# Feed-forward of a two-layer trunk: gate and up by seven half-size block products on two halves of the tokens, with block sums formed in PSUM

## The chip, the cores and the metric

One core of a Trainium2 chip. The metric is device microseconds of one execution; three runs of the kernel before gave 3630.57, 3633.33 and 3633.56, a median of 3633.33.

## The reference

Two layers over 1024 prompt frames and 8 × 16 sample frames, T = 1152 tokens of D = 1024. Layer 0 mixes tokens with RWKV-7, layer 1 with chunked band attention. After each mixer comes the part that is changed:

```python
def swiglu_ffn(x, w_gu, w_down):
    gate, up = jnp.split(x @ w_gu, 2, axis=-1)
    return (jax.nn.silu(gate) * up) @ w_down
# every layer: x += mixer(rmsnorm(x)); x += swiglu_ffn(rmsnorm(x), ...)
```

w_gu is 1024 × 5632 and w_down 2816 × 1024, all float32.

## The kernel before

Phases follow one another: front, recurrence, project, feed-forward 0, attention, feed-forward 1. Tokens lie along the free axis. Every float32 product is made of three fp32r matmuls: an operand is split into a high part (a cast, on ScalarE) and a low part (value less high part, on GpSimd for weights and VectorE for tokens), and `PASSES` multiplies high·high, high·low, low·high. A matmul has a 128 × 128 weight and 384 token columns, a third of T.

`ffn_phase` goes over the 22 blocks of 128 hidden rows, one a turn. Block 0 is plain (`plain_third`: 8 k-tiles × 3 passes × 3 thirds for gate and for up, 144 matmuls), partly while the last third of the norm is still made. In a turn g of the other 21, gate and up of one block are a 2 × 2 block product: rows are gate and up, the inner dimension is two halves of D, columns are two of the thirds. Strassen's scheme needs 7 products of 4 k-tiles × 3 passes; the last third is plain and needs 4. So a turn has 11 × 12 = 132 matmuls. Weight sums (units 2, 3, 5, 8) are made by GpSimd, token sums T1 to T4 once, in `first_turn`. Block sums are taken from PSUM to SBUF (s1, s17) and added by VectorE. Between the products stand the down projection of the block before: 8 `down_tile`s of 3 passes × 3 thirds (72 matmuls, 3 banks), each followed by one VectorE add of 128 × 1152 into H (`add`, L2393). The silus are ScalarE's, the product with up VectorE's, and the hidden block is split again (hid). The last turn has no down tiles; a tail of 24 tiles × 6 matmuls (L2255) makes the down products of the last two blocks and feeds the next phase. The order on each engine is written out by hand; engines meet by semaphores, and each runs its list in order.

Of the kernel before, what the change touches and what calls it, by code (L numbers as in the profile page):

```python
# [23 lines left out]
P = 128  # L24
# [5 lines left out]
CW = T // 3  # L30
DFF = 2816
# [1897 lines left out]
def ffn_phase(nc, t, mem, o, layer):  # L1929
# [5 lines left out]

    TURNS = HB - 1
    SA, SB, SC, TG, TU, DOWN = 0, 1, 2, 3, 4, 5
    A11, A12, A21, A22, DW = 0, 1, 2, 3, 4
    with ExitStack() as ctx:
        sem = phase_semaphores(nc, ctx, f"ffn_{layer}")  # L1940
        raw_in = [sem(f"raw_in{u}") for u in range(6)]
        u_hi, u_lo, u_done, d_hi, d_lo = (sem(x) for x in ("u_hi", "u_lo", "u_done", "d_hi", "d_lo"))
        sum_ready, sp_passed, pool_passed = sem("sum_ready"), sem("sp_passed"), sem("pool_passed")
        down_done, added = sem("down_done"), sem("added")
        s1_ready, s16_ready, s17_ready, c22_ready, c21_ready, c12_ready = (sem(x) for x in
            ("s1_ready", "s16_ready", "s17_ready", "c22_ready", "c21_ready", "c12_ready"))
        silu1_ready, silu2_ready, silu3_ready, h1_ready, h2_ready, h3_ready = (sem(x) for x in
            ("silu1_ready", "silu2_ready", "silu3_ready", "h1_ready", "h2_ready", "h3_ready"))
        hh_ready, hid_part, hid_ready, last_hi, last_lo = (sem(x) for x in ("hh_ready", "hid_part", "hid_ready", "last_hi", "last_lo"))
        gate_done, up_done, b12_read = sem("gate_done"), sem("up_done"), sem("b12_read")  # L1950
        xf_ready, tf_ready, t_hi, t_lo = (sem(x) for x in ("xf_ready", "tf_ready", "t_hi", "t_lo"))
# [8 lines left out]
        U_AT, D_AT = ((4, 5, 0, 1), (2, 3)) if layer == 0 else ((0, 1, 2, 3), (4, 5))  # L1960
        TAIL_BANK = (5, 0, 3, 4, 1, 2) if layer == 0 else (0, 3, 1, 2)
        TAIL_FREE = {0: (silu1_ready, TURNS + 2), 3: (silu3_ready, TURNS + 1), 4: (h3_ready, TURNS + 1),
                     1: (c21_ready, TURNS + 1), 2: (c12_ready, TURNS + 1), 5: (added, 8 * TURNS - 7)}
# [7 lines left out]
        def x(rows, third):  # L1971

            return tuple(mem.xs[:, part, 4 * rows:4 * rows + 4, third * CW:(third + 1) * CW] for part in range(2))
# [11 lines left out]
        def _(sp):  # L1985
# [10 lines left out]
            for q in range(2):  # L1996
                load_down(q, 0)
# [3 lines left out]
            for n, slots in ((7, (A11, A21, A22)), (8, (A12,))):  # L2001
                sp.wait_ge(u_lo, n)
                for slot in slots:
                    load_gu(slot, 2)
# [1456 lines left out]
```

## Time and profile before

| | before |
|---|---|
| median of 3 runs | 3633.33 us (3630.57 to 3633.56) |
| the profiled execution | 3635.54 us, of which the span is 3633.8 |
| PE, DVE, ACT, POOL busy | 94%, 48%, 35%, 47% of the span |
| granted TensorE clock, mean | 0.979 |
| feed-forward 1, first product to tail | 2850.27 to 3589.61 us |

PE is the TensorE matmul, PEld its weight load, DVE VectorE, ACT ScalarE, POOL GpSimd. The span is from the first to the last instruction. A busy share is an average over phases; which wait ends last in a phase is read from its rows.

### The profile page before, as it was taken

The page shows a single profiled execution, that of the slowest core. Times are in us where ns is not written, and L with a number is a line of the kernel's source. Part 1 is how long each engine was busy: PE and PEld are TensorE (multiplying, and loading weights), DVE is VectorE, ACT ScalarE, POOL GpSimd, SP SyncE. Part 2 cuts the span into 40 slices and gives each one's busy share as a digit, 9 for nine tenths or more (in the row PEclk, how much of TensorE's full clock was granted, in tenths as well). Part 3 has the DMA queues.
Part 4 walks back from the last instruction along what each step waited for, and adds up shares of the span by engine and source line. Part 5 has one row for each costly group of instructions (what it writes and reads, how often), then busy time and mean ns, then how long its engine had stood idle before and what let it go on. Part 6 is the DMA issues. An engine that isn't in the chain of part 4 may idle for free. (4 is left out here: it accounts for less than half of the span.)

```text
span 3633.8 us, 85950 instructions
## 1 busy us (share of the span) xinstructions
PE 3404.7 (94%) x34270; PEld 3155.9 (87%) x34270; DVE 1755.0 (48%) x3081; ACT 1265.7 (35%) x2607; POOL 1703.8 (47%) x1482
## 2 busy tenths in 40 slices
PE   8999878888886999999999999999989999999999
PEld 7999767777775989999999887777769899999998
DVE  6212457766663374454445533333343744545444
ACT  5212444454442132222222334444443322222224
POOL 5444355554551544445455544344433444454544
PEclk9999899999997999999999999999999999999999
DMA  4422101111102211111111134444441111111111
GB/s 151 155 87 86 65 23 38 38 45 44 42 18 92 89 44 46 46 40 51 35 52 41 60 99 101 110 102 88 105 105 65 42 48 46 40 49 37 52 38 69
DMA packets 420929, 234.94 MB, mean 65 GB/s; under 512 B 189668, under 2 KB 394228, under 8 KB 419751
## 3 DMA queue, kind: packets, MB, share of 16 engines
q1 hardware_dynamic: 417074, 216.57, 21.3%
q10 hardware_dynamic: 3572, 14.33, 1.0%
q8 instruction: 211, 3.46, 0.4%
q14 instruction: 72, 0.58, 0.1%
HBM read 188.28 MB, written 47.80 MB: 65 GB/s over the span
## 5 line engine op out<-in xcount | busy, mean ns | idle before, releaser
L2124 PE MATMUL ps<-xs,split 128*128 128x384 f32 x4032 | 738.9, 334 | 0.0
L2044 POOL TENSOR_TENSOR split<-work,split 128x512 fp32r<-128x512 f32 x320 | 409.7, 1291 | 676.2 <-ACT split L2269 676.2
L2124 PEld LDWEIGHTS ps<-xs,split 128*128 128x128 f32 x4032 | 703.0, 188 | 0.0
L2393 DVE TENSOR_TENSOR H<-ps,H 128x1152 f32<-128x1152 f32 x320 | 433.9, 1356 | 495.6 <-PE ps L2138 495.4
L2138 PE MATMUL ps<-split,split 128*128 128x384 f32 x2880 | 554.7, 336 | 11.7 <-DVE split L2467 11.0
L2138 PEld LDWEIGHTS ps<-split,split 128*128 128x128 f32 x2880 | 506.8, 189 | 13.0 <-DVE split L2467 11.7
L1228 PE MATMUL ps<-arena 64*64 64x64 f32 (+2 forms) x8800 | 428.0, 236 | 51.0 <-DVE arena L1654 15.5
L2269 ACT CAST split<-work 128x512 fp32r<-128x512 f32 x320 | 194.6, 620 | 585.5 <-PE ps L2124 349.4
L1228 PEld LDWEIGHTS ps<-arena 64*64 64x64 f32 x8800 | 323.2, 136 | 86.3 <-issue 34.0
L2939 PE MATMUL ps<-xs,split 128*128 128x384 f32 x1656 | 361.3, 355 | 2.6 <-POOL split L2853 2.6
L601 PE MATMUL ps<-mixed,wsplit_mix 128*128 128x384 f32 x1872 | 333.4, 340 | 10.6 <-DVE mixed L813 10.2
L601 PEld LDWEIGHTS ps<-mixed,wsplit_mix 128*128 128x128 f32 x1872 | 330.5, 190 | 13.2 <-DVE mixed L813 12.8
L1222 PE MATMUL ps<-arena 64*64 64x64 f32 (+2 forms) x5632 | 305.8, 241 | 28.8 <-DVE arena L1659 14.4
L2939 PEld LDWEIGHTS ps<-xs,split 128*128 128x128 f32 x1656 | 277.8, 190 | 30.1 <-issue 22.4
L1222 PEld LDWEIGHTS ps<-arena 64*64 64x64 f32 x5632 | 244.9, 134 | 63.4 <-DVE arena L1659 28.0
L2124 PE MATMUL ps<-split,split 128*128 128x384 f32 x1512 | 282.5, 336 | 0.0
L2124 PEld LDWEIGHTS ps<-split,split 128*128 128x128 f32 x1512 | 263.9, 188 | 0.0
L3102 ACT ACTIVATE work<-work,work 128x640 f32<-128x640 f32 (+3 forms) x144 | 101.1, 702 | 279.7 <-DVE work L3193 272.1
L2905 POOL TENSOR_SCALAR work<-work,work 128x640 f32<-128x640 f32 (+2 forms) x64 | 95.0, 1484 | 189.4 <-DVE work L3198 189.4
L1197 POOL TENSOR_TENSOR arena<-arena 128x320 f32<-128x320 f32 (+2 forms) x144 | 123.6, 866 | 127.2 <-PE ps L1228 102.1
L2852 POOL TENSOR_SCALAR split<-work 128x256 fp32r<-128x256 f32 x104 | 88.7, 853 | 181.2 <-DMA work<-in_attn_w_qkv 141.8
L3193 DVE CUSTOM_DVE_ANT_0 work<-ps,work 128x640 f32<-128x640 f32 (+3 forms) x144 | 91.7, 661 | 168.2 <-PE ps L2984 136.5
(316 smaller groups left out, 5189.6 us busy)
## 6 DMA issues: line engine op xcount, KB each, us to landing
work<-in_ffn_w_gu SPq DMA_DIRECT2D x168, 256.0 KB, 3.1
work<-in_ffn_w_down SPq DMA_DIRECT2D x88, 256.0 KB, 2.9
work<-in_cache_v SPq DMA_DIRECT2D x64, 256.0 KB, 3.9
work<-in_cache_k SPq DMA_DIRECT2D x256, 64.0 KB, 2.2
rkv_scratch<-lora ACTq DMA_DIRECT2D x24, 576.0 KB, 2.8
stage_mix<-in_rwkv_w_rkv SPq DMA_DIRECT2D x24, 512.0 KB, 3.7
work<-in_attn_w_qkv SPq DMA_DIRECT2D x24, 512.0 KB, 4.1
h_scratch<-H SPq DMA_DIRECT2D x2, 4608.0 KB, 12.5
```

What stands on the lines that cost most here:

```text
L601: last = pe.matmul(mem.ps[:, 4 * v + c, 0:CW], mem.wsplit[:, v, w, k * P:(k + 1) * P], mixed[part][:, k, c * CW:(c + 1) * CW], start=(k == ...
L1197: pool.tensor_tensor(m.lt[:, n % 2, 0:G, :], m.at[:, slot_of(pr, g), 0:G, 0:64], spread(m.level[:, l, :], G), ALU.mult).then_inc(lt_ready, 1)
L1222: last = pe.matmul(out[lo:hi], lhsT[lo:hi], rhs[lo:hi] if rhs is not None else eye(lo, hi), start=start, stop=stop)
L1228: last = pe.matmul(out[to:end], lhsT[lo:hi], rhs[lo:hi] if rhs is not None else eye(lo, hi), start=start, stop=stop)
L2044: pool.tensor_tensor(w[:, 1, :], UNIT_SOURCE[i], w[:, 0, :].bitcast(F32), ALU.subtract).then_inc(u_lo, 1)
L2124: last = pe.matmul(bank(b), w[:, part, k * P:(k + 1) * P], operand[xpart][:, k, :], start=(first and k == 0 and a == 0), stop=(k == 3 and ...
L2138: last = pe.matmul(bank(DOWN + c), w[:, part, (k % 4) * P:(k % 4 + 1) * P], third(mem.hid[:, xpart, :], c), start=(a == 0), stop=(a == 2))
L2269: act.copy(unit(i)[:, 0, :], UNIT_SOURCE[i]).then_inc(u_hi, 1)
L2393: dve.tensor_tensor(by3(mem.H[:, k, :]), mem.ps[:, DOWN:DOWN + 3, 0:CW], by3(mem.H[:, k, :]), ALU.add).then_inc(added, 1)
L2905: pool.tensor_scalar(pr, pr, mem.rinv[:, N % 2, 1:2], None, ALU.mult).then_inc(np_ready, 1)
L2939: last = pe.matmul(ps[:, GEMM + b, 0:CW], mem.wsplit[:, (3 * p + u) % 2, w, k * P:(k + 1) * P], mem.xs[:, part, k, c * CW:(c + 1) * CW], s ...
L3102: act.activation(pr, pr, ACT.Exp, scale=-1.0, bias=mem.mx[:, N % 2, h:h + 1], accum_out=mem.rsum[:, N % 2, h:h + 1]).then_inc(ex_ready, 1)
```

## The change

Both feed-forward phases are rewritten; nothing else is. The tokens are cut into two halves of 576, and each half product is done in two quarters of 288 columns. Gate and up of a block are then 7 products (P1 to P7, units 1 to 7) of 2 quarters × 4 k-tiles × 3 passes, 168 matmuls of 288 columns, and no plain third remains. The first two blocks are plain (`plain_third`, then `plain_block`, both with 384 columns), and 20 turns follow. In a turn P1 starts bank pair SA; ScalarE copies it from PSUM to bank pair SB (copied_b) while P2 accumulates onto SA; P3 accumulates onto SB, ScalarE copies SB to SC (copied_c), P4 accumulates onto SB, ScalarE copies SB to SA (copied_a), P5 accumulates onto SA, P6 starts SA anew, P7 accumulates onto SC. VectorE forms c22 and c12 from these and s, the copy of P6 in SBUF (p5_copied), and the hidden values as m0 (first half) and m1 (second half), both by quarters c = 0, 1. One matmul step is one k-tile of a quarter, 3 matmuls; down tiles are now 32 of 3 matmuls with 288 columns, in two banks by turns, spread over 44 of the 56 steps, and VectorE adds each to H (128 × 288). The weight units have 3 slots for 4, the down weights come in four pieces of 256 columns through one raw buffer (high_down, low_down), for two of 512. Token sums are T1 to T4 of 4 × 576, made in `plain_block`'s time in two parts each (`value`, `combine`, `t_high`, `t_low`; a part is 128 × 1152). s2_s4 and s3_s1 are the weight sums on GpSimd.

```diff
-    TURNS = HB - 1
-    SA, SB, SC, TG, TU, DOWN = 0, 1, 2, 3, 4, 5
-    A11, A12, A21, A22, DW = 0, 1, 2, 3, 4
+    TURNS = HB - 2
+    A11, A12, A21, A22 = 0, 1, 2, 3
+    GATE, UP = (0, 1, 4), (2, 3, 5)
+    SA, SB, SC, DOWN = 0, 2, 4, 6
...
+        UNIT_AT = {1: 1, 2: 2, 3: 0, 4: 1, 5: 0, 6: 2, 7: 0}
...
+            def s2_s4(g):
+                hold(pool, pool_passed, p_done, product_no(0, g))
+                hold(pool, pool_passed, sum_ready, 4 * g - 2)
+                pool.tensor_tensor(unit(3)[2], mem.raw[:, A22, :], mem.raw[:, A11, :], ALU.subtract).then_inc(sum_ready, 1)
...
+            with pool.Fori(1, TURNS) as g:
+                s2_s4(g)
+                low(3, g)
+                low(4, g)
+                low(6, g)
+                low_down(2, 4 * g + 3)
+                low(5, g)
+                low_down(3, 4 * g + 4)
                 low(1, g + 1)
...
+                s3_s1(g + 1)
+                low(7, g)
+                low_down(0, 4 * g + 5)
+                low(2, g + 1)
...
+            def down_tile(j, g):
+                m, q = down_at(j)
+                if j in (0, 4):
+                    pe.wait_ge(hid_ready, 2 * g + 1 + j // 4)
+                if j % 8 == 0:
+                    pe.wait_ge(d_lo, 4 * g + j // 8 + 1)
+                pe.wait_ge(added, TILES * g + j + 1)
+                w = mem.dring[j // 8 % 2]
                 for a, (part, xpart) in enumerate(PASSES):
...
+                    last = pe.matmul(qbank(DOWN + j % 2), w[part][:, (m % 2) * P:(m % 2 + 1) * P], quarter(mem.hid[xpart], q), start=(a == 0), stop=(a == 2))
                 last.then_inc(down_done, 1)
...
+            def plain_block():
+                step, done = 0, 0
+                for n in range(4):
+                    w, rows = mem.ring[PLAIN_AT[n]], n % 2
+                    pe.wait_ge(u_lo, n + 1)
+                    for c, b in enumerate(UP if n >= 2 else GATE):
+                        if n == 0:
+                            pe.wait_ge(gate_silu, c + 1)
+                        elif n == 2:
+                            pe.wait_ge(m1_ready if c == 2 else m0_ready, 2)
+                        for k in range(4):
+                            for a, (part, xpart) in enumerate(PASSES):
+                                last = pe.matmul(bank(b), w[part][:, k * P:(k + 1) * P], mem.xs[:, xpart, 4 * rows + k, c * CW:(c + 1) * CW],
+                                                 start=(rows == 0 and k == 0 and a == 0), stop=(k == 3 and a == 2), skip_group_check=(rows == 1))
+                            if c == 2 and k == 3:
+                                last.then_inc(p_done, 1)
+                            if n:
+                                step += 1
+                                while done < TILES * step // 36:
+                                    down_tile(done, 0)
+                                    done += 1
             def turn(g, downs):
...
+                def product(to, i, operand, first, waits, fill):
+                    nonlocal step, done
+                    pe.wait_ge(u_lo, split_no(i, g))
+                    for c in range(2):
+                        for what, value in waits:
+                            pe.wait_ge(what, value + c)
+                        for k in range(4):
+                            for a, (part, xpart) in enumerate(PASSES):
+                                last = pe.matmul(qbank(to + c), unit(i)[part][:, k * P:(k + 1) * P], operand[xpart][:, k, c * CQ:(c + 1) * CQ],
+                                                 start=(first and k == 0 and a == 0), stop=(k == 3 and a == 2), skip_group_check=not first)
+                            if k == 3:
+                                last.then_inc(p_done, 1)
+                            if fill > c and downs:
+                                step += 1
+                                while done < TILES * step // 44:
+                                    down_tile(done, g)
+                                    done += 1
+                product(SA, 1, B11, True, ((p5_copied, 2 * g - 1),), 0)
+                product(SA, 2, B21, False, ((copied_b, 2 * g - 1),), 2)
                 pe.wait_ge(t_lo, 4)
...
+                product(SB, 3, T2, False, (), 2)
+                product(SB, 4, T3, False, ((copied_c, 2 * g - 1),), 2)
+                pe.wait_ge(t_lo, 8)
+                product(SA, 5, T4, False, ((copied_a, 2 * g - 1),), 2)
+                product(SA, 6, T1, True, ((m0_ready, 2 * g + 3),), 2)
+                product(SC, 7, B22, False, (), 1)
...
+            def turn(g, last):
+                high(3, g)
+                copy_bank(SB, SA, 0, 1, c22_ready, copied_b, g)
+                hid_high(1, m1_ready, 2 * g + 2, None)
+                copy_bank(SB, SA, 1, 1, c22_ready, copied_b, g)
+                high(4, g)
+                act.wait_ge(p_done, product_no(4, g))
+                act.wait_ge(hid_ready, 2 * g + 1)
+                act.activation(by2(half(hf, 0)), mem.ps[:, SA:SA + 2, 0:CQ], ACT.Silu).then_inc(silu0_ready, 1)
+                high(6, g)
+                if not last:
+                    high_down(2, 4 * g + 3, TILES * g + 8)
+                copy_bank(SC, SB, 0, 5, c12_ready, copied_c, g)
+                copy_bank(SC, SB, 1, 5, c12_ready, copied_c, g)
+                high(5, g, True, 2 if last else 1)
+                act.wait_ge(silu0_ready, g)
+                copy_bank(SA, SB, 0, 7, None, copied_a, g)
+                if not last:
+                    high_down(3, 4 * g + 4, TILES * g + 16)
+                copy_bank(SA, SB, 1, 7, None, copied_a, g)
+                if not last:
+                    high(1, g + 1)
+                    high(7, g)
+                    high_down(0, 4 * g + 5, TILES * g + 24)
+                    p5_copy(0, g)
+                    p5_copy(1, g)
+                    high(2, g + 1)
+                    high_down(1, 4 * g + 6, TILES * g + 32)
+                    hid_high(0, m0_ready, 2 * g + 4, None)
                 else:
...
+                    high_down(2, 4 * g + 3, None, mem.down_late[0])
+                    high_last(0)
...
+            high_plain(0)
+            high_plain(1)
             norm.root(act, 2)
             for k in range(KB):
                 norm.hi(act, 2, k)
...
+            plain_silu(0, (plain_done, 1))
+            plain_silu(1, (plain_done, 2))
+            plain_silu(2, (plain_done, 5))
+            high_plain(2)
+            t_high(T3F, T3, 1)
+            hid_high(0, m0_ready, 2, None)
+            hid_high(1, m1_ready, 2, None)
+            act.wait_ge(plain_done, 6)
+            high_down(0, 1, None)
+            high_down(1, 2, None)
+            high_plain(3)
+            t_high(T2F, T2, 5)
+            high_down(2, 3, 8)
+            act.wait_ge(hid_ready, 2)
+            for c in range(3):
+                plain_silu(c, (p_done, 2))
+            high(1, 1, False, 2)
+            high_down(3, 4, 16)
+            act.wait_ge(p_done, 3)
+            t_high(T1F, T1, 3)
+            high(2, 1, False)
+            high_down(0, 5, 24)
+            act.wait_ge(t_lo, 6)
+            t_high(T4F, T4, 7)
+            high_down(1, 6, 32)
+            hid_high(0, m0_ready, 4, None)
+            with act.Fori(1, TURNS) as g:
                 turn(g, False)
             turn(TURNS, True)
...
+            def turn(g, last):
+                hid_low(1, 2 * g + 2)
+                if not last:
+                    adds(0, 20, g)
+                m0(0, g)
+                if not last:
+                    adds(20, 23, g)
+                m0(1, g)
+                if not last:
+                    adds(23, 26, g)
+                c22(0, g)
+                if not last:
+                    adds(26, 29, g)
+                c22(1, g)
+                if not last:
+                    adds(29, 32, g)
+                c12(0, g)
...
+                    hid_low(0, 2 * g + 3)
+                m1(0, g)
+                c12(1, g)
+                m1(1, g)
...
+            plain_product(0, ((plain_done, 4), (plain_done, 6)))
+            dve.wait_ge(norm.lo_done, KB)
+            value(B22, T3F)
+            value(B12, T1F)
+            for r in range(2):
+                dve.wait_ge(xf_ready, 3 + r)
+                combine(T3F, T3F, T1F, ALU.subtract, r)
+            plain_product_2(0, ((plain_done, 4), (plain_done, 6)))
+            hid_low(0, 1)
+            hid_low(1, 2)
+            value(B11, T2F)
+            for r in range(2):
+                dve.wait_ge(xf_ready, 5 + r)
+                dve.wait_ge(tf_ready, 1 + r)
+                combine(T1F, T1F, T2F, ALU.subtract, r)
+            for r in range(2):
+                dve.wait_ge(tf_ready, 3 + r)
+                combine(T2F, T3F, T2F, ALU.add, r)
+            adds(0, 2, 0)
+            dve.wait_ge(tf_ready, 6)
+            t_low(T3F, T3, 0, 1)
+            adds(2, 4, 0)
+            t_low(T3F, T3, 1, 1)
+            adds(4, 7, 0)
+            value(B21, T4F)
+            for r in range(2):
+                adds(7 + 2 * r, 9 + 2 * r, 0)
+                dve.wait_ge(xf_ready, 7 + r)
+                combine(T4F, T4F, T2F, ALU.subtract, r)
+            adds(11, 14, 0)
+            dve.wait_ge(tf_ready, 8)
+            t_low(T2F, T2, 0, 3)
+            adds(14, 17, 0)
+            t_low(T2F, T2, 1, 3)
+            adds(17, 23, 0)
+            t_low(T1F, T1, 0, 5)
+            adds(23, 25, 0)
+            t_low(T1F, T1, 1, 5)
+            adds(25, 30, 0)
+            t_low(T4F, T4, 0, 7)
+            adds(30, 32, 0)
+            t_low(T4F, T4, 1, 7)
+            plain_product(3, ((p_done, 4), (p_done, 4)))
+            plain_product_2(3, ((p_done, 4), (p_done, 4)))
+            hid_low(0, 3)
+            with dve.Fori(1, TURNS) as g:
...
```

## Rows read from the trace of the kernel before

**Rows 1.** The page, part 1: busy time, share of the span, instructions.
```profile
PE 3404.7 (94%) x34270; PEld 3155.9 (87%) x34270; DVE 1755.0 (48%) x3081; ACT 1265.7 (35%) x2607; POOL 1703.8 (47%) x1482
```

**Rows 2.** Windows view of feed-forward 1: length, busy us (instructions), PEclk, DMA share, GB/s.
```profile
2950.00:3350.00 400.00, 400.00 (x2308) 400.00 (x2307) 197.38 (x203) 99.45 (x178) 200.69 (x159) 1.00 0.15 45
```

**Rows 3.** Timeline, a silu of each turn: start, us, operation [idle before]; sixteen turns apart.
```profile
3001.52 0.53 ACT L2298 ACTIVATE work<-work 128x384 f32<-128x384 f32 x1 [1.76 <-DVE work L2431]
...
3567.59 0.52 ACT L2298 ACTIVATE work<-work 128x384 f32<-128x384 f32 x1 [1.76 <-DVE work L2431]
```

**Rows 4.** Timeline of feed-forward 1: second silu, first turn's start on PE, tail's start.
```profile
2846.53 0.49 ACT L2340 ACTIVATE work<-ps 128x384 f32<-128x384 f32 x1
...
2850.27 6.41 PE L2124 MATMUL ps<-xs,split 128*128 128x384 f32 x36
...
2862.22 3.25 PE L2138 MATMUL ps<-split,split 128*128 128x384 f32 x9 [5.54 <-DVE split L2467]
...
2865.26 2.60 PE L2124 MATMUL ps<-xs,split 128*128 128x384 f32 x12
...
3589.61 13.85 PE L2255 MATMUL ps<-split,split 128*128 128x384 f32 x78 [0.73 <-DVE split L2426]
```

**Rows 5.** Timeline of PEld: loads for 1-column matmuls, and for bf16 of 256.
```profile
2782.26 0.81 PEld L183 LDWEIGHTS ps<-ones,work 128*128 128x128 f32 x6
...
446.99 1.08 PEld L1270 LDWEIGHTS ps<-ones 128*128 128x128 bf16 x10
```

**Rows 6.** The front's loads (512, 512, 128 columns): count in 51.84:69.15, first, the one behind.
```profile
L589 PEld LDWEIGHTS ps<-mixed,wsplit_mix 128*128 128x128 f32 x90 | 14.7, 190 | 2.6
...
51.83 0.19 PEld L589 LDWEIGHTS ps<-mixed,wsplit_mix 128*128 128x128 f32 x1
...
69.16 0.09 PEld L626 LDWEIGHTS ps<-ident,shiftcol 128*9 128x9 f32 x1
```

**Rows 7.** Timeline, hand-offs from PE to DVE and from ACT to POOL.
```profile
3003.09 0.62 ACT L2269 CAST split<-work 128x512 fp32r<-128x512 f32 x1
...
3003.88 1.29 POOL L2044 TENSOR_TENSOR split<-work,split 128x512 fp32r<-128x512 f32 x1 [5.42 <-ACT split L2269]
...
3011.19 1.03 PE L2124 MATMUL ps<-xs,split 128*128 128x384 f32 x5
3011.39 1.36 DVE L2393 TENSOR_TENSOR H<-ps,H 128x1152 f32<-128x1152 f32 x1 [2.28 <-PE ps L2138]
```

**Rows 8.** Durations by width: a line each (ns min/median/max), one timeline row, one group.
```profile
L2397 DVE TENSOR_TENSOR split<-work,split x40: 941/943/949, 1347.7 to 3566.2; 128x768 fp32r<-128x768 f32 x40
...
3000.94 0.55 DVE L2431 TENSOR_TENSOR work<-ps,work 128x384 f32<-128x384 f32 x1
...
L2300 ACT CAST split<-work x40: 512/516/517, 1351.1 to 3568.7; 128x384 fp32r<-128x384 f32 x40
...
L2298 ACT ACTIVATE work<-work x40: 524/525/526, 1349.2 to 3567.6; 128x384 f32<-128x384 f32 x40
...
L2305 ACT COPY work<-ps x40: 463/470/473, 1353.1 to 3570.2; 128x384 f32<-128x384 f32 x40
...
L2853 POOL TENSOR_TENSOR split<-work,split 128x256 fp32r<-128x256 f32 x104 | 76.3, 733 | 8.7
```

**Rows 9.** DVE instructions with two SBUF inputs beside POOL's: L2421 of each turn, the start.
```profile
L2421 DVE TENSOR_TENSOR work<-work x42: 548/1640/1641, 1345.8 to 3587.8; 128x384 f32<-128x384 f32 x42
...
3032.55 1.29 POOL L2044 TENSOR_TENSOR split<-work,split 128x512 fp32r<-128x512 f32 x1 [4.88 <-ACT split L2269]
3032.62 1.64 DVE L2421 TENSOR_TENSOR work<-work 128x384 f32<-128x384 f32 x1
...
2852.38 1.91 DVE L2457 TENSOR_TENSOR work<-work 128x1536 f32<-128x1536 f32 x1
...
2852.64 2.81 POOL L2028 TENSOR_TENSOR work<-work 128x512 f32<-128x512 f32 x1
2854.39 2.67 DVE L2460 TENSOR_TENSOR work<-work 128x1536 f32<-128x1536 f32 x1
```

More of the change, by code:

```diff
@@ new lines, in ffn_phase, with x @@
+        RAW_OF = {1: A11, 2: A12, 4: A11, 5: A22, 6: A21, 7: A12}
+        unit = lambda i: mem.ring[UNIT_AT[i]]
+        split_no = lambda i, g: 7 * g + SPLIT_AT[i]
+        product_no = lambda n, g: 14 * g + (n - 10)
+        def x(rows, half):
+            return tuple(mem.xs[:, part, 4 * rows:4 * rows + 4, half * HALF:(half + 1) * HALF] for part in range(2))
+        B11, B21, B22, B12 = x(0, 0), x(1, 0), x(1, 1), x(0, 1)
+        T1, T2, T3, T4 = B12, (mem.xt[:, 0], mem.xt[:, 1]), (mem.xt[:, 2], mem.xt[:, 5]), (mem.xt[:, 4], mem.xt[:, 3])
@@ L2015, in _ @@
+            sp.wait_ge(d_lo, 4 * TURNS + 2)
+            load_down(2, TURNS)
+            for n, (i, slot) in enumerate(((4, A11), (6, A21))):
+                sp.wait_ge(u_lo, split_no(i, TURNS))
+                sp.dma_start(mem.raw[:, slot, :], down[(HB - 1) * P:HB * P, 512 * n:512 * n + 512]).then_inc(raw_in[slot], 16)
+            sp.wait_ge(d_lo, 4 * TURNS + 3)
+            load_down(3, TURNS)
             if layer == 0:
@@ L2238, in _ @@
[L2238 to L2243 removed]
+            plain_third(up_tile, UP[1], 1)
+            plain_third(gate_tile, GATE[2], 2)
+            plain_third(up_tile, UP[2], 2)
+            plain_block()
+            pe.wait_ge(gate_silu, 5)
+            with pe.Fori(1, TURNS) as g:
+                turn(g, True)
@@ L2244, in _ @@
+            turn(TURNS, False)
+            pe.wait_ge(added, TILES * TURNS + 2)
+            pe.wait_ge(hid_ready, 2 * TURNS + 2)
+            first = mem.dring + mem.down_late
             for n in range(3 * KB):
@@ new lines, in high_down, with high_last @@
+            def high_down(p, load, free, to=None):
+                act.wait_ge(down_in, 16 * load)
+                if free is not None:
+                    act.wait_ge(down_done, free)
+                w = mem.dring[p % 2] if to is None else to
+                act.copy(w[0], mem.down_raw).then_inc(d_hi, 1)
+            def high_last(n):
+                slot = (A11, A21)[n]
+                act.wait_ge(raw_in[slot], 16 * TURNS + 32)
+                act.copy(mem.last_w[n][0], mem.raw[:, slot, :]).then_inc(d_hi, 1)
```

694 lines of the change are left out of this document (251 added, 443 removed).

## The prediction

> **What bounds the kernel now.** First the busy times: PE leads with 94% of the span, DVE has 48% [rows 1]. Then the windows view of 400 us inside the second feed-forward: PE and its weight loads are busy all of it at clock 1.00, so nothing there waits for anything but PE's own pace [rows 2]. What a turn costs is therefore matmuls times pitch. Two starts of the same silu sixteen turns apart give 566.07 / 16 = 35.38 us a turn, and a turn has 132 products + 72 down matmuls = 204, so 173.4 ns each [rows 3]. Of that 384 / 2.4 GHz = 160 is column time; 13.4 ns are on top. Last, the few places where PE does wait: the start of the first turn (5.54 us, then nine matmuls in 3.04 us instead of 1.56) and 0.73 us before the tail [rows 4]. From the first product to the tail a layer takes 3589.61 − 2850.27 = 739.3 us; its 20 × 204 + 132 = 4212 matmuls are 730.5 of them, 8.8 are stalls.
>
> **The work that PE is given.** Before: 4212 matmuls of 384 columns in that stretch. After: the plain block, 4 blocks × 3 thirds × 12 = 144 of 384; then 32 down tiles of 3 in the block and in each of 19 turns, and 7 × 2 × 12 = 168 products in each of 20 turns, 1920 + 3360 = 5280 of 288 columns. Columns fall by 41,472, that is 17.3 us a layer; matmuls rise by 1212. The first 144 and the tail's 144 stay. So the whole question is the pitch of a matmul of 288 columns. The trace has none, but it bounds it:
> - A narrow matmul is held by its weight load: the six loads of 1-column matmuls start within 2782.26 to 2782.88 us (0.81 less the last one's own 0.19), the first interval behind a 384 as wide as its 0.173, the other four 0.111 each [rows 5]. 288 columns are 120 ns, so this floor is not reached.
> - The only other fp32r form is the front's triple of 512, 512 and 128. Its loads start 90 times in 17.33 us, so 0.5777 a triple; with 0.111 for the 128 the two 512s take 0.2333 each, 20 ns above 213.3 [rows 6]. The extra grows with the width: 13.4 ns at 384, 20.0 at 512. The line through both gives 173.4 − 96 × 0.468 = 128.5 ns at 288.
> - Proportion to 384 gives 130.1; a fixed 13.4 gives 133.4. Ten bf16 loads of matmuls of 256 columns start within 1.08 − 0.10 us, 0.109 apart, 106.7 + 2.2 [rows 5]; such an extra here would give 122.2.
> I take 128.5: it fits both fp32r forms. The Trainium skill (TensorE: Matmul & The Clock Gate, Back-to-back issue gap) gives N/2.4 + 2.5 ns for a warm matmul by itself, 122.5 here; the 384s at 173.4 speak against it.
>
> Without stalls: 144 × 0.1734 + 5280 × 0.1285 = 703.4 us a layer against 739.3, a gain of 35.9.
>
> **Per-turn stall.** Let E be when PE has issued a turn's last product, and each 4-k group or tile u = 0.3855 us (3 matmuls); a turn is 56 steps + 32 tiles = 88 u = 33.9 us. SA is copied to SB (copied_b) between P1 and P2: PE wants it at E + 8 u = E + 3.08. On ACT this copy stands behind silu1(1) of the turn before and high(3). Hand-off from PE's last issue to DVE is 0.20 us, from ACT to POOL 0.17, others 0.03 [rows 7]. Durations by width [rows 8]: cast 256 0.41, 576 0.68; silu 288 0.45; DVE with PSUM 288 0.45, SBUF only 576 0.75; POOL 256 0.73, 512 1.29.
> Down tile 31 issues at E − 1.54, results −1.34. high_down(1) on ACT to −0.94, low_down(1) on POOL −0.77 to −0.04. c12(0) on DVE and hid_high(0) on ACT are done by −0.35. hid_low(0) has two SBUF inputs. Here the trace matters: L2421, the only such DVE instruction of a turn that meets POOL, takes 548 ns alone and 1640 in the median, because it starts at 3032.62 under a POOL instruction that ends at 3033.84; the two exclude each other. When POOL comes second it waits as well, and gets in before DVE's next such instruction (L2028 in 2852.64 to 2855.45 behind L2457, then L2460 after it) [rows 9]. So hid_low(0) runs 0.0 to +0.72; s2 on POOL, released at +0.37, runs +0.72 to +2.01; m1(0), two SBUF inputs, waits for it, to +2.46; c12(1) to +2.83; silu1(1) to +3.30; high(3) to +3.82; the copy, PSUM to PSUM, not in the trace (PSUM to SBUF 384 is 0.47), 0.39 to +4.13. PE resumes at +4.16: it waits 1.08 us in each of 19 turns, 20.5 a layer. The Trainium skill (SBUF — State Buffer, two separate sides) says the same: an exclusive lock for the whole instruction on DVE with two SBUF inputs or GpSimd. By DVE winning m1(0) instead, the stall would be 0.3; with no collision 0.
> Every other hand-off of the turn has room: copied_c is wanted 7 u after its product, copied_a 8 u, m0 7 u, a weight unit at least 14 u after its slot comes free. DVE has 32 adds × 0.45 and 5.1 us besides, 19.5 of 35; POOL 11 × 1.29 + 4 × 0.73 = 17.1. Behind PE's wait stand only P2 and the first down tiles; hid_low(1) is in time for them (add 0 at about +6.6, wanted by tile 2 at +6.9).
>
> **The start.** Until the first product nothing changes. DVE begins with the plain product at 2847.05, after the second silu [rows 4]. Six half operands (value of B22 and B12, their difference; 1152 columns, 1.34 each, 1.27 in a row) with one POOL instruction between them end at 2856.95. ACT casts half of T3 (1.15) before hid_high(0) and (1) and high_down(0), to 2859.6; low_down(0) after hid_low(1): d_lo at 2860.9, where PE has waited since 2857.5. Then six more halves stand before the first add, with two POOL instructions let in: DVE adds at 2870.7, and PE, which has two down banks, waits at tile 2 from 2862.8 to 2871.1. After it PE has 28.2 us of work, and 1 to 2 more for a fallen clock as in [rows 4]; DVE has 30 adds and twelve halves, 28 us, and about 4 of POOL. I take the block's end at 2903.5; without stalls it is 2850.27 + 24.97 + 96 × 0.1285 = 2887.6. So 15.9 us (12 if half of the overlaps fall well, 20 if not). The tail then waits for nothing (0.7 gained, within this).
> SP's loads: four of 128 KB take the place of two of 256 in a turn; the last, A12, is issued behind load_down(1) about 7 us before the turn's end, in time.
>
> **Sum.** Per layer −35.9 + 20.5 + 15.9 = +0.5, both +1. The profiled execution took 3635.5 us (span 3633.8 and 1.7 around it), 2.2 above the median of the runs, 3633.3. So 3634 as a median. A difference under 0.2% (7.3 us) is what a measurement here can't tell from nothing.
>
> **Rivals.**
> - The pitch keeps its fixed 13.4 ns (133.4). Per layer +25.9, stalls 2.2 less: +24 a layer, 3682. For it: the extra could come in steps with 128 columns, 2 steps at 288 as at 384. Chance 0.20. In between, 130.1 gives 3650, 0.15.
> - The lock doesn't bite: m1(0) is first, or s2 comes later. Stall 0 to 0.3: 3593 to 3605 (at pitch 128.5). It decides at some 0.9 us a turn. For it: a shift of 0.3 us in hid_low(0) is enough. Chance 0.27.
> - The matmul has only the bf16 row's extra: pitch 122.2, 5280 × 6.3 ns = 33.3 a layer less, stalls 2.9 more (8 u is shorter): −30, 3573. The 384s speak against it. 0.07.
> - DVE or PE's sequencer becomes the bound in every turn (32 waits for added on two banks), or the pitch is above 135: 3700 and more. 0.08.
> - The forecast, 128.5 with 1.08: 3620 to 3650, 0.23.
>
> **Chances.** From these: faster 0.38 (lock not biting, 122.2, a little of the forecast's), same 0.20, slower 0.42 (both wider pitches, the last rival, some of the forecast's). Range 3590 to 3684: from the case without lock stalls to the fixed extra.
>
> **What the new profile would show.** Right: weight loads in a product 0.128 to 0.129 us apart; an idle of PE near 1.1 us before P2 in each turn, released by ACT's PSUM copy; m1's DVE instruction over 1.2 us in the median for one of its two halves; idles of some 3 and 8 us in the plain block, the second ended by DVE's add to H; turns of 35.0 us. Wrong: turns of 34 us or less (no lock), loads 0.133 apart, or idles spread over all down tiles (DVE bound). A start that loses less than 9 us would mean that ACT and DVE overlap better than my chain.

## The result, and the profile after

The changed kernel takes 3652.49 us (median of 4 runs, 3650.29 to 3656.64) against 3631.95 for the kernel before (4 runs, 3629.74 to 3633.56): ratio 1.0059, 95% interval 1.0046 to 1.0071. It is slower, by some 20 us, well clear of the interval. The profiled execution took 3653.95 us, span 3652.1.

The page's first part, answering [rows 1]. PE has 2424 matmuls more than before and is busy as long; DVE has gained 96 us.
```profile
PE 3407.1 (93%) x36694; PEld 3153.6 (86%) x36694; DVE 1850.6 (51%) x4051; ACT 1356.4 (37%) x2927; POOL 1686.1 (46%) x1510
```
Windows view of the steady turns, as [rows 2]:
```profile
2950.00:3350.00 400.00, 400.00 (x3007) 399.77 (x3006) 221.35 (x477) 128.89 (x277) 205.26 (x173) 1.00 0.15 44
```
PE is busy throughout, as before, with 3007 matmuls where there were 2308: 400 / 3007 is 133.0 ns each, not the forecast 128.5. And no stall of 1.08 us can stand in a turn, or PE could not be busy all of it. (The trace gives a matmul of 288 columns 0.295 us from its start, and the next one in a stream starts after 0.133, so a delay under 0.16 us does not show as idle.)

PE's timeline of feed-forward 1, the counterpart of [rows 4]: first product, first down tile, tile 2, a tile and the product behind it while the clock is low, first turn, second product of that turn, tail.
```profile
2860.92 7.45 PE L2185 MATMUL ps<-xs,split 128*128 128x384 f32 x42
...
2871.32 0.63 PE L2169 MATMUL ps<-split,split 128*128 128x288 f32 x3 [2.96 <-DVE split L2425]
...
2880.80 1.09 PE L2169 MATMUL ps<-split,split 128*128 128x288 f32 x3 [6.39 <-DVE H L2417]
...
2882.65 0.92 PE L2169 MATMUL ps<-split,split 128*128 128x288 f32 x3
2883.37 1.16 PE L2185 MATMUL ps<-xs,split 128*128 128x384 f32 x3
...
2914.67 3.34 PE L2206 MATMUL ps<-xs,split 128*128 128x288 f32 x24
2919.66 1.03 PE L2206 MATMUL ps<-xs,split 128*128 128x288 f32 x6 [1.65 <-ACT ps L2316]
...
3607.22 13.82 PE L2257 MATMUL ps<-split,split 128*128 128x384 f32 x78
```
From the first product to the tail it is 746.3 us (746.7 in layer 0), before 739.3 in both: +7.2 a layer. This stretch is the instrument of what follows. In all the profiles it repeats within 1.3 us between the two layers of a run, while the time from layer 0's tail to layer 1's first product, where nothing was changed, ranges from 801 to 810 us from one execution to the next (e4 apart, which adds matmuls there). The two layers explain 14.4 of the 18.3 us between the two spans. The other 4 are 5.3 more ahead of layer 0's first product (1310.3 against 1305.0 us; over the profiles of this study it comes at 1299.6 to 1314.6), 2.0 less between the layers and 0.7 more behind the last tail's start.

In the 746.3 us, the plain block is 53.8 and the turns 692.5. With 144 matmuls at 173.4 ns and 96 at 133.2 the block would be 37.8: it loses 16.0. The waits are the two above, three of 1.09, 0.34 and 0.24, and slow matmuls behind them. Windows view of the two stretches after the waits began:
```profile
2870.00:2880.00 10.00, 3.09 (x12) 2.61 (x12) 10.00 (x7) 1.84 (x4) 4.79 (x3) 0.60 0.17 47
2880.00:2890.00 10.00, 9.20 (x45) 9.13 (x45) 7.96 (x12) 1.85 (x3) 0.75 (x1) 0.72 0.02 6
```
PE stood still for most of the first; the granted clock is 0.60 in it and 0.72 in the next. Until 2885.8 three matmuls of 288 columns take 0.72 us from start to start (240 ns each, the columns at 1.2 GHz), after it 0.40. The 18 matmuls from 2880.80 to 2885.86 take 5.06 us instead of 2.76.

What DVE did meanwhile, its timeline: hid_low twice, B11's value (two halves), two halves each of T1 and T2, then the first adds.
```profile
2869.21 1.43 DVE L2425 TENSOR_TENSOR split<-work,split 128x576 fp32r<-128x576 f32 x2 [1.32 <-ACT split L2301]
2870.56 3.15 DVE L2492 TENSOR_TENSOR work<-xs 128x1152 f32<-128x1152 f32 x2
2873.63 6.75 DVE L2495 TENSOR_TENSOR work<-work 128x1152 f32<-128x1152 f32 x4
2880.30 0.81 DVE L2417 TENSOR_TENSOR H<-ps,H 128x288 f32<-128x288 f32 x2
```
The last place is the hand-over from turn to turn: m1(0) on DVE (L2459), s2 on POOL (L2081) and the copy to SB (L2316), first from turn 3 to 4, a steady one, then from 19 to 20, the last. Ahead of the steady one stand PE's row from the last 12 matmuls of the turn into the next, the add of the last down tile (L2417) and hid_low(0) (L2425).
```profile
3020.32 5.79 PE L2206 MATMUL ps<-xs,split 128*128 128x288 f32 x42
3020.52 0.46 DVE L2417 TENSOR_TENSOR H<-ps,H 128x288 f32<-128x288 f32 x1 [0.34 <-PE ps L2169]
...
3021.53 0.93 DVE L2425 TENSOR_TENSOR split<-work,split 128x576 fp32r<-128x576 f32 x1 [0.19 <-ACT split L2301]
...
3022.39 0.45 DVE L2459 TENSOR_TENSOR work<-work,work 128x288 f32<-128x288 f32 x1
3022.43 1.55 POOL L2081 TENSOR_TENSOR work<-work 128x512 f32<-128x512 f32 x1 [0.58 <-PE ps L2206]
...
3024.54 0.40 ACT L2316 COPY ps<-ps 128x288 f32<-128x288 f32 x1
...
3584.60 1.29 POOL L2081 TENSOR_TENSOR work<-work 128x512 f32<-128x512 f32 x1 [0.52 <-PE ps L2206]
3584.63 1.58 DVE L2459 TENSOR_TENSOR work<-work,work 128x288 f32<-128x288 f32 x1
...
3587.47 0.39 ACT L2316 COPY ps<-ps 128x288 f32<-128x288 f32 x1
```
In the steady one DVE comes 0.04 us first and m1(0) is short; s2 alone is stretched, from 1.29 to 1.55. In the last, POOL comes first, by 0.024 us before rounding, m1(0) takes 1.58, and PE waits 0.5 us. The two s2 are sixteen turns apart: 562.17 / 16 = 35.14 us a turn. The wait of 0.5 and the 1.65 in turn 1, in two layers, are all the idle time that the profile lists for the products:
```profile
L2206 PE MATMUL ps<-xs,split 128*128 128x288 f32 x3840 | 605.1, 295 | 4.3 <-ACT ps L2316 4.3
```
Below what is listed, the starts of the matmuls show one more delay: 0.05 us at the start of P2 in every steady turn.

### The profile page after: what moved, and what is told of

Same layout as the page of the kernel before. It is cut to its first block and busy times, and to the rows that moved or that the text cites. A ratio compares the mean times of both kernels' runs of the same rounds, so it can differ in the third digit from the quotient of the medians.

```text
span 3652.1 us, 95916 instructions
## 1 busy us (share of the span) xinstructions
PE 3407.1 (93%) x36694; PEld 3153.6 (86%) x36694; DVE 1850.6 (51%) x4051; ACT 1356.4 (37%) x2927; POOL 1686.1 (46%) x1510
## 5 line engine op out<-in xcount | busy, mean ns | idle before, releaser
L2417 DVE TENSOR_TENSOR H<-ps,H 128x288 f32<-128x288 f32 x1280 | 584.5, 458 | 534.8 <-PE ps L2169 534.8
L2169 PE MATMUL ps<-split,split 128*128 128x288 f32 x3840 | 722.0, 296 | 23.0 <-DVE H L2417 17.1
L2066 POOL TENSOR_TENSOR split<-work,split 128x512 fp32r<-128x512 f32 x280 | 383.6, 1375 | 498.8 <-ACT split L2283 492.1
L2169 PEld LDWEIGHTS ps<-split,split 128*128 128x128 f32 x3840 | 585.9, 189 | 27.2 <-DVE H L2417 19.0
L2206 PE MATMUL ps<-xs,split 128*128 128x288 f32 x3840 | 605.1, 295 | 4.3 <-ACT ps L2316 4.3
L2206 PEld LDWEIGHTS ps<-xs,split 128*128 128x128 f32 x3840 | 542.3, 188 | 5.9 <-issue 5.1
L2206 PE MATMUL ps<-split,split 128*128 128x288 f32 x2880 | 495.6, 296 | 0.0
L2206 PEld LDWEIGHTS ps<-split,split 128*128 128x128 f32 x2880 | 420.5, 188 | 0.0
L2990 PE MATMUL ps<-xs,split 128*128 128x384 f32 x1656 | 361.4, 355 | 2.6 <-POOL split L2904 2.6
L2990 PEld LDWEIGHTS ps<-xs,split 128*128 128x128 f32 x1656 | 277.9, 190 | 30.1 <-issue 22.4
L2283 ACT CAST split<-work 128x512 fp32r<-128x512 f32 x280 | 173.4, 619 | 228.2 <-PE ps L2206 181.7
L2071 POOL TENSOR_TENSOR split<-work,split 128x256 fp32r<-128x256 f32 x168 | 130.6, 777 | 200.1 <-ACT split L2290 199.9
```

Source lines behind the costliest of these rows:

```text
L2066: pool.tensor_tensor(w[1], frm, w[0].bitcast(F32), ALU.subtract).then_inc(u_lo, inc)
L2071: pool.tensor_tensor(w[1], mem.down_raw, w[0].bitcast(F32), ALU.subtract).then_inc(d_lo, 1)
L2169: last = pe.matmul(qbank(DOWN + j % 2), w[part][:, (m % 2) * P:(m % 2 + 1) * P], quarter(mem.hid[xpart], q), start=(a == 0), stop=(a == 2))
L2206: last = pe.matmul(qbank(to + c), unit(i)[part][:, k * P:(k + 1) * P], operand[xpart][:, k, c * CQ:(c + 1) * CQ], start=(first and k == 0 ...
L2283: act.copy(w[0], w[2] if i == 3 else mem.raw[:, RAW_OF[i], :]).then_inc(u_hi, inc)
L2417: dve.tensor_tensor(h, qbank(DOWN + j % 2), h, ALU.add).then_inc(added, 1)
```

## The experiments

Stretches are first product to tail, layers 0 and 1; block is the part up to the first turn. The changed kernel has 746.7 and 746.3, block 54.2 and 53.8. A steady turn is the distance between the first products of two turns away from both ends: 35.14 us in the changed kernel. The theory: the loss against the kernel before is DVE's work at the start; the pitch took the gain that should have paid for it; the collision at the turn's end is real but missed by a hair. Rivals stand with each run.

**e1: only the order in the plain block.** Short form of the edit:
```
-            value(B11, T2F)
-            ... T1F, T2F: four halves
-            adds(0, 2, 0)
+            for n, half_work in enumerate(work):      # 18 halves
+                half_work()
+                adds(at, TILES * (n + 1) // 18, 0)
```


> The changed kernel with only DVE's order in the plain block different: the 18 half-operand instructions of the token sums (1.27 to 1.7 us each) and the 32 adds of the down tiles take turns, one or two adds behind each half, instead of six halves ahead of the first add. In the changed kernel PE waits 6.39 us at tile 2, and the clock falls behind it. Theory 'order': that wait and the fallen clock are there because the adds stand behind six halves; they go, and the block ends 8 to 10 us earlier in each layer: 3633 to 3637 us in all. Theory 'load': DVE has more to do in the block than PE (32 adds of 0.41, 18 halves of about 1.35, and what POOL holds it up, together some 42 us against PE's 37.8), so the waits are only spread over more tiles: the block ends at most 3 us earlier, 3646 to 3652 us. I expect the second.

3641.7 us (3638.3 to 3644.47; before 3635.9), ratio 1.0012, 1.0002 to 1.0021. Stretches 739.0 and 739.8, blocks 47.5 and 48.3. The block gives back 6 us, between the two theories (8 to 10, and at most 3), so the time lies outside both ranges. The wait at tile 2 is gone; the one at tile 0, ahead of the reordered part, is still 2.93 us, and the clock still falls behind it (0.91 and 0.92 in the two windows from 2860 to 2880). The windows view of e1 shows what is left:
```profile
2880.00:2890.00 10.00, 9.39 (x57) 8.23 (x55) 10.00 (x12) 2.80 (x7) 7.90 (x5) 1.00 0.06 15
2890.00:2900.00 10.00, 8.22 (x48) 7.16 (x49) 10.00 (x15) 3.14 (x4) 3.98 (x3) 1.00 0.08 26
```
DVE is busy 10.00 of 10 us in both and PE is not: there DVE has more to do than PE. So six of the 16 us were order. Of the ten that are left, 2.9 are the wait at tile 0, which this run did not touch; the others go with DVE's full queue and the low clock behind tile 0, and no run separates these two.

**e2: the start's sums spread out.** The core of the edit (the buffers of the T's are renumbered, since the norm's own lie under two of them):
```
             for k in range(1, KB):
                 norm.add(dve, 2, k)
+            value(B11, V11)
             norm.inverse(dve, 2)
+            value(B21, T4F)
             norm.split(dve, 2)
...
+            turn(1, False, True)      # adds with t_low(T1), t_low(T4) between them
-            with dve.Fori(1, TURNS) as g:
+            with dve.Fori(2, TURNS) as g:
```


> The changed kernel with the start's token sums taken apart: the values of B11 and B21 (four halves) are formed while DVE waits for the norm of the last third (it idles 3.1 and 4.6 us there); the halves that are left take turns with the adds; the low parts of T1 and T4 (four halves) and ScalarE's high part of T4 move into turn 1, ahead of product 5; ScalarE copies the high halves of hid and the first down unit before the high part of T3. Arithmetic and amount of work unchanged. Theory 'load': ten to twelve halves are left in the block, DVE fits in PE's time, the waits at tiles 0 and 2 (2.96 and 6.39 us) and the cold stretch go: 12 to 16 us less in each layer, 3620 to 3629 us in all, faster than the kernel before. Rival: the work only moves, and PE waits as long in turn 1 for T2's or T4's low part: 3640 us and more.

3629.67 us (3627.25 to 3634.58), ratio 0.9982, 0.9972 to 0.9991: 6 us below the kernel before. Stretches 734.4 twice, blocks 41.0. The block gave 13 us back, one of which turn 1 took again (0.41 and 0.37 us of waits). Both waits at tiles 0 and 2 are gone, and the clock is 1.00. Twelve us a layer are at the low end of what was expected (12 to 16), and the time is 0.7 us above its range. The halves that moved ahead of the first product cost nothing there: from the first matmul of `plain_third` to the first product it is 28.5 us, as in the changed kernel.

**e3: no sums.** T1 to T4 replaced by B12, B21, B22, B11; the sums left out.
```
-        T1, T2, T3, T4 = B12, (mem.xt[:, 0], mem.xt[:, 1]), ...
+        T1, T2, T3, T4 = B12, B21, B22, B11
```


> The changed kernel without the token sums: the four sums T1 to T4 are not computed, the products take B12, B21, B22 and B11 in their place. Left out are 22 DVE halves and 8 ScalarE halves in each layer and PE's waits for them; matmuls, adds and copies are all there. Theory: all of the start's loss over its matmuls (16.0 us in the plain block and 1.65 in turn 1) is due to these sums: 15 to 17.6 us less in each layer, 3617 to 3623 us. Rival: a part of it is the down tiles' own hand-off over two PSUM banks or the late silus: then above 3630 us. If the steady turns lose nothing, they stay at 264 matmuls of 133.3 ns.

3616.26 us (3615.25 to 3617.78), ratio 0.9943, 0.9926 to 0.9959. Stretches 727.9 twice, blocks 38.1: nearly the 37.8 of bare matmuls. PE waits for down tiles nowhere. The whole loss at the start belongs to the sums, and the two PSUM banks of the down tiles cost nothing by themselves. The stretch is 18.6 us shorter, one more than the expected 15 to 17.6: the steady turns are 35.05 us long instead of 35.14, and no run shows why. It also marks the floor: with the sums free the change would gain 11.4 us a layer, at this pitch.

**e4: distance of loads by width.**
```
+            if layer == 1:
+                for width in WIDTHS:
+                    for i in range(48):
+                        pe.matmul(mem.ps[:, DOWN, 0:width], gate_tile[...], mem.xs[:, i % 2, i % 8, 0:width], ...)
```


> The changed kernel with 12 x 48 extra fp32r matmuls on PE ahead of the second feed-forward's first product, 48 in a row of each width from 256 to 512 columns into one PSUM bank that nobody reads: it measures the distance of weight loads by width. Rows of this case: 133.3 ns at 288 and 173.4 at 384 (13.3 above the columns' time at 2.4 GHz in both), 233.3 at 512 (20 above). Theory 'fixed': 13.3 above the columns at every width up to some point between 384 and 512 (120.0 at 256, 140.0 at 304, 146.7 at 320, 160.0 at 352), and the 20 at 512 belong to the front's triple or to a step. Theory 'line', on which the prediction stood: it is refuted at 288; if it held elsewhere, 256 would be near 113. Time: about 90 to 100 us more than the changed kernel.

One run of 3754.39 us. Timeline of PEld, two loads to a row; loads 3 and 45 of a width are 42 apart. 288 columns, 384, then single loads 4 and 46 of 512.
```profile
2847.49 0.33 PEld L2231 LDWEIGHTS ps<-xs,split 128*128 128x128 f32 x2
...
2853.02 0.32 PEld L2231 LDWEIGHTS ps<-xs,split 128*128 128x128 f32 x2
...
2875.18 0.36 PEld L2231 LDWEIGHTS ps<-xs,split 128*128 128x128 f32 x2
...
2882.47 0.36 PEld L2231 LDWEIGHTS ps<-xs,split 128*128 128x128 f32 x2
...
2923.87 0.19 PEld L2231 LDWEIGHTS ps<-xs,split 128*128 128x128 f32 x1
...
2933.41 0.19 PEld L2231 LDWEIGHTS ps<-xs,split 128*128 128x128 f32 x1
```
5.53 / 42 is 131.7 ns at 288, 7.29 / 42 is 173.6 at 384, 9.54 / 42 is 227.1 at 512. By such pairs, over the columns at 2.4 GHz:

| columns | 256 | 272 | 288 | 304 | 320 | 352 | 384 | 416 | 448 | 480 | 496 | 512 |
|---|---|---|---|---|---|---|---|---|---|---|---|---|
| ns | 120.0 | 125.2 | 131.7 | 137.9 | 146.7 | 160.0 | 173.3 | 188.3 | 206.7 | 216.7 | 223.1 | 227.1 |
| over | 13.3 | 11.9 | 11.7 | 11.2 | 13.3 | 13.3 | 13.3 | 15.0 | 20.0 | 16.7 | 16.4 | 13.8 |

The extra is 11 to 13 ns from 256 to 384 and does not fall steadily with the width. At 512 it is 13.8, not the 20.0 that the prediction had drawn its line through. At 288 it is 131.7 ns, 1.5 less than in the kernel's turns; no run shows what the turns add.

**e5: a gap of one small operation on DVE.**
```
                     hid_low(0, 2 * g + 3)
+                    dve.tensor_scalar(free[:, 0:1], mem.vec[:, 0, 0:1], 1.0, None, ALU.mult)
                 m1(0, g)
```


> The changed kernel with one 1-column DVE operation (some 0.1 us) between hid_low(0) and m1(0) in every turn. In the changed kernel POOL's s2 is released about 0.3 us behind PE's last issue E, while hid_low(0) runs; DVE's m1(0) follows hid_low(0) at once and runs first, s2 only after it. Theory 'the loser of the collision is decided by the gap': with a gap POOL gets in, s2 runs from about E + 0.6 to E + 1.9, m1(0) waits for it (over 1.2 us in the trace), and c12(1), silu1(1), high(3) and the copy to SB follow as the prediction laid them out: PE waits 0.8 to 1.1 us before P2 in each of 19 turns, 30 to 42 us in all, a ratio of 1.014 to 1.018 to the kernel before (the changed kernel: 1.006). Rival: the order of the two engines is decided otherwise (by which was asked first, or DVE always first): m1(0) stays short and the time stays within 3 us of the changed kernel.

3656.69 us (3647.92 to 3659.57; before 3634.97), ratio 1.0058, 1.0042 to 1.0073: as the changed kernel. Stretches 746.4 and 746.3; a steady turn takes 35.20 us, 0.06 more, and the blocks happen to be 1 us shorter. Timeline of a steady hand-over of e5:
```profile
3050.55 0.44 DVE L2459 TENSOR_TENSOR work<-work,work 128x288 f32<-128x288 f32 x1
...
3050.53 1.61 POOL L2081 TENSOR_TENSOR work<-work 128x512 f32<-128x512 f32 x1 [0.58 <-PE ps L2206]
```
The gap is 0.07 us wide and doesn't turn the order: m1(0) starts 0.02 us behind s2's recorded start and still takes 0.44. It doesn't tell the theories apart, so the edit was repeated with a wider gap.

**e8 and e9: a wide gap, and the same with the copy first.** Four such operations; e9 also swaps `high(3, g)` and the first `copy_bank(SB, SA, 0, ...)`.

> The changed kernel with four 1-column DVE operations (0.14 us for one, the next starts 0.07 behind it) between hid_low(0) and m1(0) in every turn instead of the one of the run before. In that run s2 and m1(0) still started within 0.05 us of each other, and m1(0) stayed at 0.44 us; only in the last turn, where s2 came 0.03 us ahead in the changed kernel and 0.09 in that run, m1(0) took 1.58 and 1.52 us and PE waited about 0.5 us. Theory 'who arrives first has the memory': with 0.2 us more DVE is second in every turn, m1(0) is over 1.2 us in all 40 turns, and PE waits about 0.5 us in each of 19: the stretch from the first product to the tail grows by 9 to 11 us a layer, to about 756 us (the changed kernel: 746.5), 18 to 22 us in all. Rival: DVE has precedence at the end of an instruction of its own: m1(0) stays short and the stretch stays at 746.5.

> The kernel of e8 with ScalarE's first copy to SB ahead of high(3) in every turn. If e8's wait of 0.5 us comes down the chain s2, m1(0), c12(1), silu1(1), high(3), copy, the cast taken out of it (0.60 us) ends it: a stretch of 743 to 744 us, as with one small operation and the same swap (743.2). If the stretch stays near 756, the wait sits elsewhere.

e8: 3673.87 us (3670.95 to 3675.38; before 3630.73), ratio 1.0117, 1.0094 to 1.0141. Stretches 760.0 and 758.9. Timeline of a steady turn of e8, and what the copies are waited for:
```profile
3030.83 1.29 POOL L2081 TENSOR_TENSOR work<-work 128x512 f32<-128x512 f32 x1 [0.58 <-PE ps L2206]
3031.03 1.40 DVE L2459 TENSOR_TENSOR work<-work,work 128x288 f32<-128x288 f32 x1
...
  ACT ps L2316: 24.7, 40
```
Now POOL is first in every turn and m1(0) waits for it. Of the 24.7 us, 1.65 a layer are turn 1's as before, so PE idles (24.7 − 3.3) / 38 = 0.56 us at each later hand-over. What the turn loses is more, since the next matmul of a stream starts 0.133 us behind the one before and idle is counted only from 0.295: a steady turn takes 35.89 us, 0.75 more than in the changed kernel, all of it at the start of P2. That is the chain that the prediction laid out, at some two thirds of its price of 1.08. The stretch grows by 13 us, as 18 such turns give, and not by the expected 9 to 11. e9: 3662.09 us (3661.55 to 3666.97), ratio 1.0091, 1.0066 to 1.0115; stretches 754.7 and 754.5. Idle time listed for the copies falls from 24.7 to 1.5 us, so the chain did run through high(3); but only 5 of the 13 us come back, where 12 were expected and a stretch of 743 to 744. A steady turn takes 35.66 us, 0.58 more than with the same swap and no stall (35.08, e7). By the starts of the matmuls 0.33 of these are still lost at the start of P2: the chain without high(3) is late too. The other 0.25 are lost at tile 2, where hid_low(1), late and 1.58 us long, holds up the first adds:
```profile
3025.92 0.83 PEld L2206 LDWEIGHTS ps<-xs,split 128*128 128x128 f32 x6 [0.30 <-issue]
...
3026.95 1.58 DVE L2425 TENSOR_TENSOR split<-work,split 128x576 fp32r<-128x576 f32 x1 [0.85 <-ACT split L2301]
...
3028.45 0.81 DVE L2417 TENSOR_TENSOR H<-ps,H 128x288 f32<-128x288 f32 x2
3028.95 0.30 PEld L2169 LDWEIGHTS ps<-split,split 128*128 128x128 f32 x2 [0.22 <-DVE H L2417]
```
So there is a second branch, by hid_low(1) and the adds. In e8 it costs nothing, since PE comes later to tile 2 there; it shows when the first one is shortened.

**e7: one small operation, and the copy first.** The swap of e9 on e5.

> The kernel of e5 with one more edit: ScalarE's first copy to SB stands ahead of high(3) in every turn. If e5's stall comes down the chain s2, m1(0), c12(1), silu1(1), high(3), copy, this takes 0.62 us (the cast of 512 columns) off it: 0.1 to 0.5 us are left in a turn, 4 to 19 us over the changed kernel in all, a ratio of 1.007 to 1.011. If e5's stall, where there is one, sits elsewhere (in hid_low(1) and the adds behind it, say), the swap changes nothing and this run equals e5.

3649.32 us (3641.64 to 3653.3), ratio 1.0034, 1.0024 to 1.0045. Stretches 743.1 and 743.2. There was no stall in e5 to take away, so the expectation's condition didn't hold; the swap is worth 3.2 us a layer by itself: 1.4 are waits of the first and last turn (4.3 us in all become 1.5), the rest is a delay in every steady turn (35.20 us in e5, 35.08 here). By the starts of the matmuls it is 0.11 us at the start of P2, too short for the profile to list as idle: also without a stall, P2 waits for the copy behind high(3).

**e6: e2 with its idle places taken.** t_high(T2) halves around high_down(2, 3); T1's and T4's parts earlier in turn 1; copy to SB ahead of high(3).

> The kernel of e2 with its remaining idle places taken: ScalarE copies the third down unit between the two high halves of T2 (PE waited 1.35 us for that unit), the low halves of T1 and the high and low halves of T4 come earlier in turn 1 (0.41 and 0.37 us of waits and a slack stretch of about 1.2 us there), and the first copy to SB stands ahead of high(3) in every turn (0.60 us of wait in turn 1). If these waits are what separates e2 (41.0 us of plain block and 693.4 us of turns and tail wait in a layer) from e3 (38.0 and 689.9), 2.5 to 4 us less in each layer: a ratio of 0.9960 to 0.9968 to the kernel before (e2: 0.9982). Rival: DVE is full in this stretch (32 adds and 12 to 14 halves) and each wait taken away comes back behind another add: within 1 us of e2 a layer, 0.9977 to 0.9984.

3622.92 us (3620.43 to 3631.58), ratio 0.9961, 0.9947 to 0.9974. Stretches 730.9 twice, blocks 40.0, turns 690.9; the products wait for nothing, the down tiles 1.9 us a layer. This is what was expected (2.5 to 4 us less a layer, ratio 0.9960 to 0.9968). It is the fastest kernel of the study that does all the work, 12 us under the kernel before and 3 us a layer above the floor of e3.

**r1: the changed kernel again,** on the chip of e8 and e9.

> The changed kernel itself beside the two kernels above on the same chip: a ratio of 1.004 to 1.007 to the kernel before, and a stretch from the first product to the tail of 746 to 747 us in both layers, whatever the other stages do.

3645.98 us (3641.64 to 3650.0), ratio 1.0042, 1.0030 to 1.0054. Stretches 746.5 and 746.2. The loss is 15 to 20 us in the two measurements, and 14 of it are in the two stretches.

## Why the prediction was right, and where it was not

3634 was forecast, 3652.5 came: inside the range, off by 18.5. That it is no further off is luck: of three terms two failed, in opposite directions, by 24.9 and 18.3 us a layer, and only the start was right. Slower had the largest chance, 0.42, beside a forecast of no change. Per layer:

| term | forecast | measured | how |
|---|---|---|---|
| matmuls, and the old 8.8 of stalls gone | −35.9 | −11.0 | 144 × 173.4 + 5280 × 133.2 ns = 728.3, against 739.3 |
| stall at the turn's end | +20.5 | +2.2 | 1.65 in turn 1, 0.5 in turn 20 |
| start | +15.9 | +16.0 | 53.8 − 37.8 |
| sum | +0.5 | +7.2 | the stretches: +7.4 and +7.0 |

(133.2 is the turns' 692.5 less 2.2 of waits, over 5184 matmuls.)

**The pitch.** The step that failed is "The extra grows with the width: 13.4 ns at 384, 20.0 at 512. The line through both gives 173.4 − 96 × 0.468 = 128.5 ns at 288". The reading of the front's triple was right. Timeline of its loads: 52.17 stands with the start of a second 512, 52.40 with that of the 128, and the second load of that row follows after 0.11 (0.30 less its own 0.19).
```profile
52.17 0.19 PEld L589 LDWEIGHTS ps<-mixed,wsplit_mix 128*128 128x128 f32 x1
...
52.40 0.30 PEld L589 LDWEIGHTS ps<-mixed,wsplit_mix 128*128 128x128 f32 x2
```
Over the 30 triples of [rows 6] the distances are 235, 233 and 109 ns in the mean, so the 512s do take 20 to 22 ns over their columns there; the 233 stands between the matmuls' own starts too. What did not hold is to carry this to a stream of one width. In e4's stream a 512 takes 227.1 ns; through 173.3 and 227.1 the same line gives 133 ns at 288, where the turns have it. Why a 512 takes 6 to 8 ns more in the front's triple, no run shows. The rival "keeps its fixed 13.4" named the size, and had 0.20. The Trainium skill (TensorE: Matmul & The Clock Gate, Back-to-back issue gap) also states some 131 ns for a sustained matmul of 512 columns; this case's fp32r matmuls take 227.1.

**The lock.** The chain was right in form: e8 shows each link. The steps that failed are two starts in it, "hid_low(0) runs 0.0 to +0.72" and "s2 on POOL, released at +0.37". E is the start of the matmul behind the turn's last one; in the steady hand-over that is shown it is 3020.32 + 12 × 0.133 = 3021.92. There hid_low(0) starts at −0.39, beside POOL's low_down(1), and lets m1(0) start at +0.46, 0.26 earlier than forecast; s2 starts at +0.51, 0.14 later. Either shift alone would have left s2 first, by 0.21 or 0.09 us. A down tile's add on DVE follows the start of PE's next matmul after 0.20 us, s2 after 0.51. The program has two waits ahead of s2, each with an increment, and the loop's jump, and the prediction costed the hand-off of a single wait [rows 7]; for the last turn, outside the loop, POOL idles 0.52 before it instead of 0.58, s2 starts 0.07 earlier, and it wins. That the waits are what delays s2 is argued, not shown. So s2 and m1(0) came within 0.05 us of each other, and the stall hung on that; the prediction's own rival, "a shift of 0.3 us in hid_low(0) is enough" or "s2 comes later", named both.

The Trainium skill (SBUF — State Buffer, two separate sides) says that whichever starts first has the port for its whole instruction; with 0.2 us between them (e8) the runs agree. In e5's steady turns s2's start is recorded 0.02 us ahead of m1(0)'s, and m1(0) was the short one all the same. Over the 418 hand-overs of the eleven profiles with the new turn there is one dividing line: m1(0) is short wherever s2's recorded start is at most 0.021 us ahead, and waits wherever it is 0.023 us or more ahead. Why the line is not at zero stays open.

**The start.** Right in size and place: waits of 2.96 and 6.39 us at the two places named (3.4 and 8.3 were forecast), the fallen clock, the block's end after 53.8 us (53.2). Its cause is shown by e3, the sums. By e1 six us are order; the ten left are the wait at tile 0 and DVE's load, which no run separates further.

**The cases.** Lock and pitch are independent, and the prediction gave each its case but never crossed them. "Fixed 13.4" with "the lock doesn't bite" makes −35.9 + 25.9 + 15.9 = +5.9 a layer, 3645: that is what happened, but for 1.3 us a layer more and what lies outside the stretches. From the two chances, 0.20 × 0.27, it would have had some 0.05; it was not listed at all.

**What the profile was to show.** Of the signs named for wrong, loads 0.133 apart appear, and the idle of 1.1 us before P2, named for right, does not; "idles of some 3 and 8 us in the plain block, the second ended by DVE's add to H" was right. The "turns of 35.0 us" came true as well, with 35.14, but for another reason: forecast were 33.9 of matmuls and 1.08 of stall, and measured are 264 matmuls at 133.1 ns. The length of a turn by itself could not tell the two apart.

## What to carry to other kernels

Smaller matmuls bring less than their columns say: here the columns of the stretch fell by 2.6% and the matmuls' time by 0.3% (730.5 to 728.3 us), since there are more of them and each keeps its extra. Vector work of a start-up stage that exceeds the matmuls beside it cost twice here, by the wait and by the clock after it (18 matmuls in 5.06 us instead of 2.76); put it into idle places before the stage and behind it (e2, e6), since reordering alone (e1) returned a good third. When two unknowns are independent, cross them in the list of cases, and don't carry an extra that was read in a mixed group over to a stream of one width. And when a loss is read from idle times, compare it with the length of the turn: in e8 the idle time was 0.56 us and the loss 0.75.

## What the runs showed of the hardware that was not expected

- The extra of an fp32r matmul over its columns isn't smooth in the width: 11.2 to 13.3 ns from 256 to 384 columns, 20.0 at 448, 13.8 at 512 (e4). For the same 512 columns it is 20 to 22 ns in the front's triple of 512, 512 and 128.
- Which of DVE and POOL wins SBUF turned on hundredths of a us: DVE at the steady hand-overs (s2's median 1552 ns), POOL at the last (m1(0) 1.58 us). In 418 hand-overs DVE won up to a recorded lead of POOL of 0.021 us and lost from 0.023 us on.
- The clock fell after waits of PE of 2.93 and 2.96 us: three matmuls of 288 columns then took 0.72 us, against 0.40 at full clock. After e2's wait of 1.35 us it did not fall.
- A PSUM to PSUM copy of 288 columns on ScalarE takes 384 ns in the median, near the 0.39 that the prediction took from a copy to SBUF.
